# A one-layer HGRN2 / convolution / mixture-of-experts step: the order of the first loads and the place of the parameter turns

## The reference

```python
h = rmsnorm(x, norm_mix)
q, fz, inp, g, u_a, u_b = split(h @ w_in)              # w_in: 1024 x 3072
f = lb + (1 - lb) * sigmoid(fz)                        # lb from a softmax of hgrn_lb_logits
o, s_new = hgrn2_scan(q, log(f), 1 - f, inp, s0)       # 4 heads of 128, chunks
o = rmsnorm_per_head(o) * silu(g)
c = silu(layernorm(causal_conv31(u_a * sigmoid(u_b)) + conv_b))
x = x + concat(o, c) @ w_out
x = x + moe(rmsnorm(x, norm_ffn))                      # top 4 of 32 experts, 1024 wide, clamped SwiGLU
x = x + sigmoid(rmsnorm(x, norm_ple) @ w_ple_gate) * (p @ w_ple)
y = rmsnorm(x, norm_final)
```

## Time and profile before

| | |
|---|---|
| median of 3 runs | 1221.03 us (1220.55 to 1221.03) |
| the profiled execution's own time | 1219.33 us |
| its span | 1217.5 us |
| TensorE busy | 1125.7 us (92%) |
| VectorE, ScalarE, GpSimd busy | 387.3, 232.8, 39.5 us |
| DMA | 430.73 MB, mean 354 GB/s |
| chain that ended last, by engine | PE 68%, DMA 26%, DVE 3%, ACT 1% |
| mean granted clock of TensorE | 0.983 |

### The profile page before, as it was taken

One profiled execution on the slowest core, in us unless ns is written; L12 is line 12 of the kernel. 1 busy time (PEld: TensorE's weight loads), 2 busy tenths in 40 slices (PEclk: granted clock), 3 DMA queues, 4 the chain that ended last, 5 costly groups with the idle time before them and its releaser, 6 DMA issues.

```text
span 1217.5 us, 14744 instructions
## 1 busy us (share of the span) xinstructions
PE 1125.7 (92%) x5871; PEld 462.0 (38%) x5871; DVE 387.3 (32%) x838; ACT 232.8 (19%) x370; POOL 39.5 (3%) x23
## 2 busy tenths in 40 slices
PE   5999989899999999999989898989898989899986
PEld 4775655433333333333323232323232323233333
DVE  5568975621313212121212121212130303031234
ACT  3531114412020101111111111111202020211124
POOL 3340000100000000000000000000000000000000
PEclk9998999699999999999999999999999999999998
DMA  9913121699999999999999999999999999999911
GB/s 288 365 37 139 43 104 42 239 386 430 428 427 428 430 428 428 428 430 427 429 428 429 428 428 428 430 428 429 428 429 428 429 428 430 428 428 428 427 44 39
DMA packets 44057, 430.73 MB, mean 354 GB/s; under 512 B 4885, under 2 KB 8933, under 8 KB 19359
## 3 DMA queue, kind: packets, MB, share of 16 engines
q1 hardware_dynamic: 39016, 425.42, 83.7%
q10 hardware_dynamic: 5015, 4.95, 1.2%
HBM read 428.53 MB, written 1.83 MB: 353 GB/s over the span
## 4 chain that ended last, share of the span: by engine, by line
PE 68%; DMA 26%; DVE 3%; ACT 1%; issue 1%; SPq 0%; ACTq 0%; DVEq 0%
PE ps L779 34%; DMA ring<-in_w_gate_up 24%; PE ps L480 7%; PE ps L470 5%; PE ps L739 5%; PE ps L704 4%; PE ps L798 4%; DMA ring<-in_w_down 2%; PE ps L714 2%; PE ps L788 1%; PE ps L504 1%; PE ps L747 1%; PE ps L544 1%; PE ps L562 1%; PE ps L706 1%
## 5 line engine op out<-in xcount | busy, mean ns | idle before, releaser
L779 PE MATMUL ps<-ring,arena 128*64 128x512 f32 x2048 | 466.7, 598 | 19.4 <-DMA ring<-in_w_gate_up 19.4
L798 PE MATMUL ps<-ring,arena 128*64 128x512 f32 x1024 | 232.3, 598 | 30.8 <-DMA ring<-in_w_down 13.6
L779 PEld LDWEIGHTS ps<-ring,arena 128*64 128x64 f32 x2048 | 136.5, 137 | 296.0 <-issue 255.7
L798 PEld LDWEIGHTS ps<-ring,arena 128*64 128x64 f32 x1024 | 68.5, 137 | 171.2 <-issue 113.6
L1694 DVE TENSOR_TENSOR acc<-ps,acc 128x512 f32<-128x512 f32 x64 | 44.2, 691 | 212.8 <-PE ps L739 212.8
L1580 DVE CAST arena<-cst 96x128 bf16 (+1 forms) x17 | 3.8, 222 | 273.0 <-PE ps L779 273.0
L1104 ACT COPY arena<-ps 128x512 f32<-128x512 f32 x32 | 18.7, 586 | 328.9 <-PE ps L788 328.9
L480 PE MATMUL ps<-ring,arena 128*128 128x512 f32 x140 | 64.3, 615 | 1.1 <-DVE arena L1472 1.1
L470 PE MATMUL ps<-arena,ring 128*128 128x288 f32 x256 | 64.2, 410 | 0.7 <-DVE arena L1249 0.7
L1599 DVE TENSOR_TENSOR arena<-ps,par 128x256 f32<-128x256 f32 x68 | 25.5, 417 | 121.5 <-PE ps L779 118.4
L739 PE MATMUL ps<-arena 128*128 128x512 f32 x128 | 63.5, 619 | 0.0
(11 more groups left out here) (267 smaller groups left out, 799.9 us busy)
## 6 DMA issues: line engine op xcount, KB each, us to landing
ring<-in_w_gate_up SPq DMA_DIRECT2D x128, 2048.0 KB, 24.4
ring<-in_w_down SPq DMA_DIRECT2D x64, 2048.0 KB, 23.1
ring<-in_w_in SPq DMA_DIRECT2D x5, 2048.0 KB, 20.5
ring<-in_w_out SPq DMA_DIRECT2D x2, 2048.0 KB, 15.8
ring<-in_w_in SPq DMA_DIRECT2D x2, 1024.0 KB, 11.9
arena<-in_w_ple_gate ACTq DMA_DIRECT2D x2, 768.0 KB, 5.6
arena<-in_w_ple_gate ACTq DMA_DIRECT2D x1, 1280.0 KB, 10.2
acc<-in_x_prompt SPq DMA_DIRECT2D x2, 512.0 KB, 4.5
```

The costliest lines, as they stand in the source:

```text
L779: t = mm(ps[h * 64:h * 64 + 64, G + 2 * e + g, :], xT[:, 2 * kk + c, e * 64:e * 64 + 64], w[:, c, lo:lo + 512], start=False, stop=(kk == 3 ...
L798: t = mm(ps[n * 64:n * 64 + 64, PP + e, :], hidT[:, 4 * e + c, half * 64:half * 64 + 64], w[:, c, n * 512:(n + 1) * 512], start=(half == 0 ...
```

## The change

SyncE's queue now begins with block 0 of x, the identity alone (`cst[:, 0:C_TRI]`, its own semaphore `id_in`), blocks 1 and 2, norm_mix alone (`mix_rows`, `mix_in`), the first half of unit 0, the rest of the constants, the ten parameter loads as before, the second half of unit 0, the biases, and the other units. ScalarE first takes the square root of a cleared `hss` (which brings the table in), and issues its six loads behind the roots of all three blocks. TensorE turns norm_mix alone first, then the frames, the first chunk of columns, the other parameters (`turn_params`), and the other three chunks. VectorE copies norm_mix alone before the six gain multiplications, and the rest of the parameters behind them. PSUM bank 1 takes the turned parameters, so the turns of p, which write that bank, wait for `lb_sub`.

```diff
@@ block.sync
             for b in range(NB):
                 src, r = ROW_OF[b]
                 sp.dma_start(X2[0:ROWS[b], b, :], src[0, r:r + ROWS[b], :]).then_inc(S[f"x_in{b}"], 16)
-            sp.dma_start(cst[:, :], a["consts"]).then_inc(S["cst_in"], 16)
+                if b == 0:
+                    sp.dma_start(cst[:, 0:C_TRI], a["consts"][:, 0:C_TRI]).then_inc(S["id_in"], 16)
+            sp.dma_start(mix_rows, a["norm_mix"].rearrange("l (c p) -> (l c) p", p=P)).then_inc(S["mix_in"], 16)
...
+            w_in(0, 0, W // 2, S["w_in_head"])
+            sp.dma_start(cst[:, C_TRI:C_END], a["consts"][:, C_TRI:C_END]).then_inc(S["cst_in"], 16)
             for name, n in (("norm_mix", 8), ("norm_ffn", 8), ("norm_ple", 8), ("hgrn_lb_logits", 8),
...
-            w_in(0, 0, W // 2, S["w_in_head"])
+            w_in(0, W // 2, W, full[0])
             for r in range(3):
                 sp.dma_start(braw[r * E:(r + 1) * E, :], a["b_gate_up"][0]).then_inc(S["raw_in"], 16)
-            w_in(0, W // 2, W, full[0])
@@ block.tensor
-            pe.wait_ge(S["cst_in"], 16)
-            pe.wait_ge(S["par_in"], 16 * 10)
-            tr(ps[:, 0, 0:R_END], par_rows[0:R_END, 0:P], cs(C_ID, R_END, R_END))
-            tr(ps[:, 0, 64:64 + CW * H], par_rows[0:CW * H, P:2 * P],
-               cs(C_ID, CW * H, CW * H))
-            for r in range(2):
-                t = tr(ps[:, 0, 256 + r:256 + DC:2], gain_rows[:, r:2 * P:2], cs(C_ID, 4, 4))
-            t.then_inc(S["par_mm"], 1)
+            pe.wait_ge(S["id_in"], 16)
+            pe.wait_ge(S["mix_in"], 16)
+            tr(ps[:, 1, 0:DC], mix_rows, cs(C_ID, DC, DC)).then_inc(S["mix_mm"], 1)
...
+            def turn_params():
+                pe.wait_ge(S["cst_in"], 16)
+                pe.wait_ge(S["par_in"], 16 * 10)
+                tr(ps[:, 1, DC:R_END + DC], par_rows[0:R_END, 0:P], cs(C_ID, R_END, R_END))
+                tr(ps[:, 1, 64:64 + CW * H], par_rows[0:CW * H, P:2 * P],
+                   cs(C_ID, CW * H, CW * H))
+                for r in range(2):
+                    t = tr(ps[:, 1, 256 + r:256 + DC:2], gain_rows[:, r:2 * P:2], cs(C_ID, 4, 4))
+                t.then_inc(S["par_mm"], 1)
+
             def turn_frames():
 
+                pe.wait_ge(S["lb_sub"], 1)
                 pe.wait_ge(S["p_in"], 16 * NB)
...
-            columns(0)
+            columns(0, [0])
+            turn_params()
+            columns(0, [1, 2, 3])
             turn_frames()
@@ block.scalar
-            act.dma_start(crow, a["cache_conv"][0, 0]).then_inc(S["aux_in"], 16)
...
+            act.wait_ge(S["hss_ready"], 1)
+            fn(hrs[:, 0:1], hss[:, 0:1], ACT.Sqrt)
             for b in range(NB):
                 act.wait_ge(S[f"x_in{b}"], 16)
...
             root(0, 2)
+
+            act.dma_start(crow, a["cache_conv"][0, 0]).then_inc(S["aux_in"], 16)
...
@@ block.vector
+            V.memset(hss, 0.0).then_inc(S["hss_ready"], 1)
             zero_rest(X2[:, 2, :]).then_inc(S["zero_ready"], 1)
-
-            V.memset(hss, 0.0)
...
-            dve.wait_ge(S["par_mm"], 1)
-            V.tensor_copy(par[:, 0:R_END], ps[:, 0, 0:R_END])
...
+            dve.wait_ge(S["mix_mm"], 1)
+            link(V.tensor_copy(par[:, R_MIX:R_MIX + DC], ps[:, 1, 0:DC]))
...
             for b in range(NB):
                 columns_with_gain(hT, b, "xt_mm", "ht_ready", (2, 3, 4, 5, 6, 7), R_MIX)
+
+            dve.wait_ge(S["par_mm"], 1)
+            V.tensor_copy(par[:, DC:R_END], ps[:, 1, 2 * DC:R_END + DC])
...
```

More of the change, by code:

```diff
@@ L204, in program @@
         par_rows = cacc[:, 0, 0:2 * P]
+        mix_rows = cacc[0:DC, 2, 0:P]
         gain_rows = cacc[0:4, 1, 0:2 * P]
@@ L323, in _ @@
         def _(sp):
+            at_row = 0
+            rows = par_rows[:, 0:P]
             for b in range(NB):
@@ L326, in _, with w_in @@
                 sp.dma_start(X2[0:ROWS[b], b, :], src[0, r:r + ROWS[b], :]).then_inc(S[f"x_in{b}"], 16)
-            sp.dma_start(cst[:, :], a["consts"]).then_inc(S["cst_in"], 16)
-            at_row = 0
-            rows = par_rows[:, 0:P]
+                if b == 0:
+                    sp.dma_start(cst[:, 0:C_TRI], a["consts"][:, 0:C_TRI]).then_inc(S["id_in"], 16)
+            sp.dma_start(mix_rows, a["norm_mix"].rearrange("l (c p) -> (l c) p", p=P)).then_inc(S["mix_in"], 16)
+            def w_in(u, lo, hi, done):
+                sp.dma_start(slot(u).rearrange("p (c n) -> p c n", c=DC)[:, :, lo:hi],
+                             a["w_in"][0, :, GROUPS[u] * W + lo:GROUPS[u] * W + hi].rearrange(
+                                 "(c p) n -> p c n", p=P)).then_inc(done, 16)
+            w_in(0, 0, W // 2, S["w_in_head"])
+            sp.dma_start(cst[:, C_TRI:C_END], a["consts"][:, C_TRI:C_END]).then_inc(S["cst_in"], 16)
             for name, n in (("norm_mix", 8), ("norm_ffn", 8), ("norm_ple", 8), ("hgrn_lb_logits", 8),
@@ L911, in _ @@
             root(0, 2)
+            act.dma_start(crow, a["cache_conv"][0, 0]).then_inc(S["aux_in"], 16)
+            for b in range(NB):
+                src = a["p_prompt"][0, 0, b * P:(b + 1) * P, :] if b < 2 else a["p_sample"][0, 0]
+                act.dma_start(pr[0:ROWS[b], b, :], src).then_inc(S["p_in"], 16)
+            act.dma_start(Ss.rearrange("p (h v) -> p h v", h=H),
+                          a["state_hgrn"][0, 0].rearrange("h k v -> k h v")).then_inc(S["aux_in"], 16)
+            act.dma_start(brow, a["b_router"].broadcast_to([P, E])).then_inc(S["aux_in"], 16)
             act.wait_ge(S["lb_sub"], 1)
@@ L1254, in _ @@
                 columns_with_gain(hT, b, "xt_mm", "ht_ready", (2, 3, 4, 5, 6, 7), R_MIX)
+            dve.wait_ge(S["par_mm"], 1)
+            V.tensor_copy(par[:, DC:R_END], ps[:, 1, 2 * DC:R_END + DC])
+            link(V.tensor_copy(par[:, R_END:R_END + CW * H], ps[:, 1, 64:64 + CW * H]))
+            link(V.tensor_copy(par[:, R_XG:R_XG + DC], ps[:, 1, 256:256 + DC]))
+            link(V.tensor_tensor(lb_m, pcol(R_LB, H), pcol(R_LB + H, H), ALU.max))
+            V.tensor_tensor(blocks(lb_e, 2), blocks(pcol(R_LB, 2 * H), 2),
+                            lb_m.unsqueeze(1).broadcast_to([P, 2, H]), ALU.subtract).then_inc(S["lb_sub"], 1)
             dve.wait_ge(S["act"], 1)
```

13 lines of the change are left out of this document (2 added, 11 removed).

## The result

The changed kernel took 1215.8 us (median of 5 runs, 1213.63 to 1218.59), the kernel before, run beside it, 1221.03 (5 runs, 1218.83 to 1222.33): a ratio of 0.9958, with an interval of 0.9938 to 0.9979. That is faster by more than the 0.2% bound, and 1215.8 lies under the predicted range: the gain was larger than forecast. One kernel's own runs spread over 5 to 10 us, so from here on means stand beside the medians.

A forecast was written before the change was run, and what follows sets the result against it. The prediction saw the end bound by an expert weight stream that waits for TensorE, whose columns would start 3.5 us earlier, less 0.8 for parameter turns: 1221.03 - 2.7 = 1218.3 us, range 1216.9 to 1221.2.

The forecast's parts named there:

- ScalarE: Opening, path of the frames: early square-root table removes two 1.28 us table loads; last normalised block 2.0 us earlier.
- The drain behind a table load: ScalarE table switch: the skill's drain makes it 2.66 us; by that page the sum would be some 1.4 us better.
- VectorE: Opening: six gain multiplications take 3.1 us and end at 13.7, so columns start 3.5 us earlier.
- Parameter turns: Now between column products 8 and 9, at about 17.6, they lengthen TensorE's row by 0.8 us (0.7 to 1.04).
- Frame turns: TensorE's turns behind unit 0's columns, which need ScalarE's loads, were expected at 30.4 with those loads in time.
- The loads: Opening: head of w_in lands at 13.2, just ahead of columns at 13.7; it and the later landings cost nothing.
- the rival of late loads: ScalarE's loads behind a full w_in queue come late: 22 us makes 1222.2; chance 0.08, other costly late landings included.
- GpSimd's cover: Raw biases moved behind 1 MB: GpSimd done 3 us later, at 41.2, against a use at 43.9; no cost.
- The clock rival: TensorE starts columns at the lower clock, half pace for 3.8 us: costs 1.9 us, gain 0.8, 1220.2; chance 0.34.
- The step that failed: Between columns and expert stage: an earlier TensorE start moves the weight stream and the end by the same amount.
- a start that moves without it: Sign of being wrong: columns start earlier but the first expert load, expected 2.7 us earlier, does not move.
- The forecast sum of 2.7: Opening: -3.5 us from earlier columns, +0.8 for turns put inside them; ends of the sum -2.3 and -3.4.

The follow-up runs named there:

- ScalarE's part alone: Kernel before with only the early square-root table and ScalarE's six loads moved behind the roots: 1218.7 us (12 runs), 0.9976.
- the two held back kernels: Kernel before with SyncE's first load waiting for one or two VectorE memsets: 1223.11 us (1.0019) and 1222.31 us (1.0011).
- the changed kernel held back: Changed kernel with SyncE's first load waiting for one or two VectorE memsets: 1218.48 us (0.9982) and 1219.64 us (0.9984).
- the loads alone: Changed kernel with ScalarE as it was before (six loads first, two table loads): 1218.61 us (12 runs), 0.9983.

## Why the prediction was wrong, step by step

**ScalarE: right in kind, better for block 0, worse for block 1.** Both table loads left the path. Block 0 was squared at 4.04 (predicted 4.7). Block 1 landed at 7.2, not 6.2: the identity between the two issues was named and costed at nothing, and the run without it shows 1.4 us. The third square came at 8.51 instead of 7.3. Squaring block 0 early gained little, since VectorE takes block 1's mean before it scales block 0: the frame turns ahead of the columns began at 9.53, where 8.4 was forecast. The drain behind a table load that the Trainium skill states (ScalarE: Activation LUTs, "What ACT_TABLE_LOAD costs") isn't in this trace either: the next instruction starts at 2.01, 0.01 us behind the load's end.

**VectorE: right.** Its path took 2.89 us for the six multiplications (3.1 predicted) and the columns followed 0.04 us behind; all of the miss, 14.64 for 13.7, is block 1's, whose lateness put the third square 1.2 back.

**Parameter turns: right.** 0.78 us, predicted 0.8; at 20.96 instead of 17.6, by the later start and the slow columns. Frame turns at 33.57 instead of 30.4, for the same two reasons.

**The loads: all in time.** The head of w_in landed at 10.7, 3.9 us ahead. That it could be the last to arrive in the kernel before (17.81 in its second trace) was not seen. The router bias took 16.0 us instead of 7.7, the last block of p 12.6 instead of 7.1: the condition of the rival of late loads was half true, and 5 us of cover remained. GpSimd's cover shrank from 8.41 to 3.04 (2.7 worked out).

**The clock rival came true in some traces, and was priced rightly.** The first chunk took 6.32, 5.99 and 6.20 us in three traces of kernels with the new order (1.9 us was the price; 2.0 to 2.4 came), but 4.15 in four others without idle products in the opening. The old order has it at times too: unit 0 took 17.77 us with ScalarE's part alone and 17.36 and 17.29 in the two held back kernels, against 15.79. So it isn't tied to the new order; whether the change makes it more frequent, these few traces can't say. At 0.34 it was not overrated; that it would come and the kernel would still gain more than the forecast was in no case.

**The step that failed is the one that the sum took for granted:** that "whatever lets TensorE begin its columns earlier should move the stream and the end by the same amount, if nothing between them has a date of its own". That it reaches the end held: the fit gives 0.82 to 0.97 per us of start, the changed kernel held back 1.0. That it is the whole gain did not. What was missing is a term for the stages between the columns and the experts. TensorE is at the lower clock for some 40 us of each run (30.7 and 23.9 of them between 95 and 240 us in the traced pair), and with the change it is 6 us less. The kernel with the loads alone shows the missing term by itself: next to nothing gained by the start, 2.8 us gained in all. In the traced pair the opening's gain was lost by 95 us (slow columns, 2.4), and 3.1 us came between 95 and 240 us. The prediction said that the first expert load would be 2.7 us earlier, and named a start that moves without it as a sign of being wrong; in this pair the load was 0.5 later (94.86 for 94.33), and the later expert loads 2.5 earlier. The forecast sum of 2.7 is not confirmed by the 2.7 of the held-back kernel: the start moved 2.6 and not 3.5, and the turns' 0.8 come off that. The range was too narrow below since no case held a gain outside the opening.

**What stays open:** why this order of the opening leaves 6 us less low time over 100 us later, and how much of the 1.6 us that is. Both patterns of low stretches were seen in traces of both orders. Of the seven traces with the new order and no idle products ahead of 210 us six had the pattern that begins with 1.00, and one had 0.90 and 0.83; of the six with the parameter turns in front one had it. That is a link, not a cause; it wasn't tried which of the moved turns and loads makes it.

## What to carry to other kernels

A wait removed at the head of a chain reaches the end nearly in full, even 1200 us later, where the stages hand over by semaphores. But read the granted clock in each stage as well, in more than one trace: here low stretches of 40 us a run, at 0.1 to 0.3 us for each of them, came to as much as the change or more, moved from run to run and made one pair of traces misleading. Where an engine waits for another in a stage with a low clock, idle products on TensorE are a cheap test (3.9 us here in one kernel, 0.7 in the other). They must be sized by their duration where they stand (five took 6.89 us in the opening, 1.38 each), or they push what they were to speed up.

## What the runs showed of the hardware

- A load of 64 KB issued between two x loads of 512 KB made the second land 1.4 us later (5.58 us from an issue at 1.65, against 4.65 from 1.18).
- The six loads on ScalarE's queue (16 to 256 KB) took 8.6 to 16.0 us when issued behind w_in loads on SyncE's, and 3.2 to 7.7 before.
- The record of the granted clock reads 1.00 in the opening while the same eight products take 6.32 us or 4.15: there the durations tell the pace, not the clock's record.
- The low time of a kernel, 44 or 38 us, moved by less than 1 us when the first load was held back by 1.4 or 2.6 us. Five idle products took 18 us of it away in the kernel before, 8 in the changed one.
